# State-space stage: the heads' products in pairs on the two column halves, and another order of ScalarE's and VectorE's work behind each group

## The reference, cut to what matters

```python
CB = einsum('btgn,bsgn->btsg', C_c, B_c)
y_intra = einsum('btsg,btsgh,bsgh,bsghp->btghp', CB, L, dt_c, x_c)
y_inter = einsum('btgn,bghpn,btgh->btghp', C_c, state, exp(cum))
...
y = y + D_skip * xh
y = y * silu(z)
y = y * rsqrt(mean(y * y over the group) + EPS) * g_out
h = h + y @ w_out
```

## Time and profile before

| what | value |
|---|---|
| median of 3 runs | 1914.03 us (1911.9 to 1917.88) |
| the profiled execution | 1913.78 us, of which its span is 1912.0 us |
| busy in the span | PE 1800.4 us (94%), DVE 989.7 (52%), ACT 789.6 (41%), POOL 711.9 (37%) |
| the state-space stage | from 80 to about 520 us of the span |
| chain that ended last | PE 76%, DVE 14%, ACT 5%, issue 3% |

### The profile page before, as it was taken

The page is one execution under the profiler, slowest core; times in us unless marked ns, Lnnn a source line. Parts: engine busy times, 40 slices in busy tenths (PEclk is TensorE's granted clock), DMA queues, the critical chain, the costliest instruction groups (busy, mean ns, idle before and its releaser), DMA issues.

```text
span 1912.0 us, 24962 instructions
## 1 busy us (share of the span) xinstructions
PE 1800.4 (94%) x8907; PEld 1426.5 (75%) x8907; DVE 989.7 (52%) x1549; ACT 789.6 (41%) x1341; POOL 711.9 (37%) x795
## 2 busy tenths in 40 slices
PE   5999898998899988999999999999989989999998
PEld 3877776766677655777877878888778768888887
DVE  5658578366634686345656846667631342122122
ACT  4435334344445666335553235544542342223231
POOL 0644444332435210531112432222324545555553
PEclk8999999999999899999999999999999989999999
DMA  5332331211122200211105832121123223333333
GB/s 164 94 101 88 97 113 56 65 49 62 44 81 78 61 23 12 80 45 34 34 23 181 262 108 55 34 56 45 45 67 92 85 72 100 93 99 99 97 90 99
DMA packets 238794, 152.04 MB, mean 80 GB/s; under 512 B 7997, under 2 KB 223046, under 8 KB 238694
## 3 DMA queue, kind: packets, MB, share of 16 engines
q1 hardware_dynamic: 225894, 125.54, 23.1%
q10 hardware_dynamic: 12800, 25.17, 4.0%
HBM read 148.59 MB, written 2.10 MB: 79 GB/s over the span
## 4 chain that ended last, share of the span: by engine, by line
PE 76%; DVE 14%; ACT 5%; issue 3%; DMA 1%; POOL 0%; SPq 0%; DVEq 0%; ACTq 0%; POOLq 0%
PE ps L636 19%; PE ps L640 19%; PE ps L637 19%; PE ps L2004 2%; DVE xs L1241 2%; PE ps L1986 1%; PE ps L1487 1%; PE ps L1519 1%; PE ps L667 1%; PE ps L1993 1%; PE ps L2447 1%; PE ps L918 1%; DVE al L748 1%; DVE queries L1756 1%; DVE mod_part L1262 1%
## 5 line engine op out<-in xcount | busy, mean ns | idle before, releaser
L586 POOL TENSOR_TENSOR wl<-raw,wh 128x256 fp32r<-128x256 f32 (+1 forms) x775 | 688.3, 917 | 1137.9 <-ACT wh L599 1137.9
L636 PE MATMUL ps<-ah,wh 128*128 128x512 f32 (+1 forms) x1208 | 493.3, 408 | 32.6 <-DVE al L748 13.3
L640 PE MATMUL ps<-ah,wl 128*128 128x512 f32 (+1 forms) x1208 | 477.0, 395 | 0.0
L637 PE MATMUL ps<-al,wh 128*128 128x512 f32 (+1 forms) x1208 | 476.3, 394 | 0.0
L599 ACT ACTIVATE wh<-raw 128x1024 fp32r<-128x1024 f32 (+1 forms) x220 | 230.8, 1049 | 345.2 <-PE ps L640 330.8
L636 PEld LDWEIGHTS ps<-ah,wh 128*128 128x128 f32 (+1 forms) x1208 | 229.0, 190 | 104.5 <-issue 39.9
L640 PEld LDWEIGHTS ps<-ah,wl 128*128 128x128 f32 (+1 forms) x1208 | 228.6, 189 | 52.5 <-issue 0.8
L637 PEld LDWEIGHTS ps<-al,wh 128*128 128x128 f32 (+1 forms) x1208 | 229.5, 190 | 46.3 <-issue 1.2
L636 PE MATMUL ps<-bh,wh 128*128 128x512 f32 (+1 forms) x588 | 235.8, 401 | 14.1 <-DVE resid L1352 9.9
L637 PE MATMUL ps<-bl,wh 128*128 128x512 f32 (+1 forms) x588 | 232.1, 395 | 0.0
L640 PE MATMUL ps<-bh,wl 128*128 128x512 f32 (+1 forms) x588 | 231.8, 394 | 0.1
(11 more groups left out here) (372 smaller groups left out, 2621.9 us busy)
## 6 DMA issues: line engine op xcount, KB each, us to landing
raw<-w_mlp SPq DMA_DIRECT2D x64, 512.0 KB, 3.8
raw<-w_in SPq DMA_DIRECT2D x52, 512.0 KB, 3.8
raw<-ssm_w_in SPq DMA_DIRECT2D x40, 512.0 KB, 3.8
ada_late<-w_ada ACTq DMA_DIRECT2D x16, 1024.0 KB, 6.5
ada_raw<-w_ada ACTq DMA_DIRECT2D x16, 512.0 KB, 3.6
raw<-ssm_w_out SPq DMA_DIRECT2D x16, 512.0 KB, 3.4
raw<-mla_w_in SPq DMA_DIRECT2D x11, 512.0 KB, 3.9
raw<-mla_w_out SPq DMA_DIRECT2D x8, 512.0 KB, 3.5
```

Source lines behind the costliest of these rows:

```text
L586: nc.gpsimd.tensor_tensor(wl[:, s, part], raw[:, s, part], wh[:, s, part].bitcast(F32), ALU.subtract).then_inc(lo_ready, LOW_PIECES * (par ...
L636: nc.tensor.matmul(dst, w_hi[k], x_hi[k], start=k == 0, stop=False)
L637: nc.tensor.matmul(dst, w_hi[k], x_lo[k], start=False, stop=False)
L640: ins = nc.tensor.matmul(dst, w_lo[k], x_hi[k], start=False, stop=k == n - 1)
```

## The change

The outputs of two heads are made together: one call for each pair, at odd h, whose five steps each issue the product of the even head and then that of the odd head, so that neighbouring products use different column halves. `seg` and `carry` get a second pair of buffers, in memory that is free in these groups. ScalarE's exponentials of pair p now wait for the outputs of pair p - 2. VectorE takes pair (h - 3) / 2 at h = 3, 5 and 7, instead of pair h / 2 - 1 at h = 2, 4 and 6.

Behind a group, ScalarE first copies P6's result to `zs` as it is and makes the high part of P8's weights, then the squares and the rstd; Silu of the copy comes later, in place; the gate of P7's result and the split behind it move ahead of the four high parts. VectorE's residual add of an output product's first half waits for that half alone (`half_done`), and in the last group the first of these adds stands ahead of the wait for the rstd. At the start of the stage one semaphore is replaced by another.

```diff
@@ pe_mamba
-            def outputs(g, h):
-                pair, part = h // 2, slice(HP * (h % 2), HP * (h % 2) + HP)
...
-                pe.wait_ge(sem("mix_ready"), g * GH + h + 1)
...
+            def outputs(g, pair):
+                b = 6 + pair % 2
+                pe.wait_ge(sem("y_taken"), g * 4 + max(pair - 1, 0) + AHEAD)
+                pe.wait_ge(sem("mix_ready"), g * GH + 2 * pair + 2)
+                for step in range(5):
+                    for two in range(2):
+                        h, part = 2 * pair + two, slice(HP * two, HP * two + HP)
...
+                ins_.then_inc(sem("y_ready"), 1)
@@ output on TensorE
+                    if c == 0:
+                        ins_.then_inc(sem("half_done"), 1)
@@ heads on TensorE
-                    outputs(g, h)
+                    if h % 2:
+                        outputs(g, h // 2)
@@ heads on ScalarE
-                    act.wait_ge(sem("y_ready"), g * GH + max(h - 1, 0) + AHEAD)
+                    act.wait_ge(sem("y_ready"), g * 4 + max(h // 2 - 1, 0) + AHEAD)
@@ act_mamba
             for g in range(GROUPS - 1):
                 heads(g)
+                act.wait_ge(sem("gated"), g * 4 + 1)
+                act.wait_ge(unit_done, unit("ssm", g, 6) + 1 + CREDIT)
+                nc.scalar.activation(zs[:, 0], bank(0), ACT.Copy).then_inc(acc_free[0], 1)
+                split_ahead(act, "ssm", g, 6)
                 for p in range(4):
                     square(g, p)
-                split_ahead(act, "ssm", g, 6)
                 scale(g)
-                gate("ssm", g, g + 1, 0)
+                act.wait_ge(acc_free[0], g * 9 + ACC0["ssm"][0] + 5)
+                nc.scalar.activation(zs[:, 0], zs[:, 0], ACT.Silu)
+                gate("ssm", g, g + 1, 1)
+                split_ahead(act, "ssm", g, 7)
                 for p in range(4):
                     high(g, p)
-                gate("ssm", g, g + 1, 1)
-                split_ahead(act, "ssm", g, 7)
@@ heads on VectorE
-                    if h % 2 == 0 and h:
-                        take(h // 2 - 1)
+                    if h % 2 and h >= 3:
+                        take((h - 3) // 2)
@@ normed on VectorE
+                if between is not None:
+                    between(0)
                 dve.wait_ge(sem("grstd"), g * 2 + 2)
                 for p in range(5):
-                    if between is not None and 1 <= p <= 2:
-                        between(p - 1)
+                    if between is not None and p == 2:
+                        between(1)
@@ output on VectorE
-                dve.wait_ge(unit_done, unit(stage, i, n0 + w) + 1 + CREDIT)
                 for c in range(2):
+                    dve.wait_ge(*((unit_done, unit(stage, i, n0 + w) + 1 + CREDIT) if c else
+                                  (sem("half_done"), 4 * (i if stage == "ssm" else GROUPS - 1) + w + 1)))
```

More of the change, by code:

```diff
@@ L268, in _build @@
                    for k, a in enumerate((fixed.at, fixed.at + DC * P * 4, b_at + 14 * T * 4))]
+        cl_at = fixed.at
         cl = fixed("cl", [P, DC, CTX], F32R)
@@ L495, in _build, with of_head @@
         carry = r("carry", [P, 2, SSM_CHUNK])
+        segs, carries = [seg], [carry]
+        for name, a in (("bl", b_at + 8 * T * 4), ("cl", cl_at)):
+            r2 = Region(a, a + 4 * T * 4)
+            segs.append(r2("seg_" + name, [P, 2, 2 * CW]))
+            carries.append(r2("carry_" + name, [P, 2, SSM_CHUNK]))
+        def of_head(buffers, g, h):
+            pair, two = divmod(h, 2)
+            return buffers[0 if pair % 2 == 0 else 1 if g < 2 else 2][:, two]
         r2 = Region(b_at + 4 * T * 4, b_at + 8 * T * 4)
@@ L908, in exponents @@
                 ins_.then_inc(sem("sums_ready"), 1)
-            def outputs(g, h):
-                pair, part = h // 2, slice(HP * (h % 2), HP * (h % 2) + HP)
-                b, own = 6 + pair % 2, slice(h * HP, (h + 1) * HP)
-                if h % 2 == 0:
-                    pe.wait_ge(sem("y_taken"), g * 4 + max(pair - 1, 0) + AHEAD)
-                pe.wait_ge(sem("mix_ready"), g * GH + h + 1)
[L917 to L924, removed]
+            def outputs(g, pair):
[5 more added lines that the diff above has]
+                        h, part = 2 * pair + two, slice(HP * two, HP * two + HP)
+                        own, z = slice(h * HP, (h + 1) * HP), of_head(segs, g, h)
+                        if step == 0:
+                            nc.tensor.matmul(bank(b, part, slice(0, W0)), xdt[:, 0, own], z[:, 0:W0], start=True, stop=False)
+                        elif step == 1:
+                            nc.tensor.matmul(bank(b, part, slice(P, W0)), xdt[:, 1, own], z[:, W0:CW], start=False, stop=True)
+                        elif step == 2:
+                            nc.tensor.matmul(bank(b, part, slice(W0, T)), xdt[:, 2, own], z[:, CW:CW + W0], start=True, stop=False)
+                        elif step == 3:
+                            nc.tensor.matmul(bank(b, part, slice(W0 + P, T)), xdt[:, 3, own], z[:, CW + W0:2 * CW], start=False, stop=False)
+                        else:
+                            ins_ = nc.tensor.matmul(bank(b, part, slice(W0, T)), state[:, own], of_head(carries, g, h), start=False, stop=True)
+                ins_.then_inc(sem("y_ready"), 1)
@@ L1003, in act_mamba @@
         def act_mamba(act):
[L1005 removed]
+            act.wait_ge(acc_free[0], ACC0["dt"][0] + 2)
             nc.scalar.activation(dt_e[:], dt_u[:], ACT.Abs).then_inc(sem("dt_act"), 1)
@@ L1048, in heads @@
                         k, cols = j // 2, (slice(0, W0), slice(W0, CW))[j % 2]
-                        nc.scalar.activation(seg[:, h % 2, k * CW + cols.start:k * CW + cols.stop], bank((b0, b1)[k])[:, cols],
+                        nc.scalar.activation(of_head(segs, g, h)[:, k * CW + cols.start:k * CW + cols.stop], bank((b0, b1)[k])[:, cols],
                                              ACT.Exp, bias=ncum[:, j, g * GH + h:g * GH + h + 1])
-                    nc.scalar.activation(carry[:, h % 2].rearrange("p (k n) -> p k n", n=P), ps[:, b0:b1 + 1, CW:T],
+                    nc.scalar.activation(of_head(carries, g, h).rearrange("p (k n) -> p k n", n=P), ps[:, b0:b1 + 1, CW:T],
                                          ACT.Exp).then_inc(sem("seg_ready"), 1)
@@ L1187, in dve_mamba @@
             dve.wait_ge(unit_done, unit("dt", 0, 0) + 1 + CREDIT)
-            nc.vector.tensor_scalar(dt_u[:], bank(0, slice(0, NH)), ssm_a[:, 0:1], None, ALU.add).then_inc(sem("dt_u"), 1)
-            dve.wait_ge(sem("dt_u"), 1)
-            dve.sem_inc(acc_free[0], 1)
+            nc.vector.tensor_scalar(dt_u[:], bank(0, slice(0, NH)), ssm_a[:, 0:1], None, ALU.add).then_inc(acc_free[0], 1)
+            dve.wait_ge(acc_free[0], ACC0["dt"][0] + 2)
             dve.wait_ge(sem("dt_act"), 4)
@@ L1300, in take @@
                 def take(pair):
-                    dve.wait_ge(sem("y_ready"), g * GH + 2 * pair + 2 + AHEAD)
+                    dve.wait_ge(sem("y_ready"), g * 4 + pair + 1 + AHEAD)
                     nc.vector.scalar_tensor_tensor(xs[:, pair], xs[:, pair], dcol[:, g * 4 + pair:g * 4 + pair + 1], bank(6 + pair % 2),
@@ L1310, in heads @@
                     dve.wait_ge(sem("seg_ready"), g * GH + h + 1)
-                    nc.vector.tensor_tensor(seg[:, h % 2], seg[:, h % 2], cb[:], ALU.mult)
-                    nc.vector.tensor_tensor(carry[:, h % 2], carry[:, h % 2], ct[:, SSM_CHUNK:T], ALU.mult).then_inc(sem("mix_ready"), 1)
-                    if h % 2 == 0 and h:
-                        take(h // 2 - 1)
+                    z, c = of_head(segs, g, h), of_head(carries, g, h)
+                    nc.vector.tensor_tensor(z, z, cb[:], ALU.mult)
+                    nc.vector.tensor_tensor(c, c, ct[:, SSM_CHUNK:T], ALU.mult).then_inc(sem("mix_ready"), 1)
+                    if h % 2 and h >= 3:
+                        take((h - 3) // 2)
                     if g < CTX_BLOCKS // 2:
@@ L1392, in last_of_group @@
             def last_of_group(c):
-                if c:
-                    dve.wait_ge(unit_done, unit("ssm", GROUPS - 2, 13) + 1 + CREDIT)
+                dve.wait_ge(*((unit_done, unit("ssm", GROUPS - 2, 13) + 1 + CREDIT) if c else (sem("half_done"), 4 * (GROUPS - 1))))
                 nc.vector.tensor_tensor(resid[:, 6 + c], resid[:, 6 + c], bank(c), ALU.add).then_inc(acc_free[c], 1)
```

## The result

| | before | changed | ratio, 95% interval |
|---|---|---|---|
| median | 1913.68 us (1911.9 to 1917.88, 4 runs) | 1886.88 us (1883.59 to 1887.34, 4 runs) | 0.9853, 0.9834 to 0.9873 |
| profiled execution | 1913.78, span 1912.0 | 1883.59, span 1881.8 | |

The change gained 26.8 us by the medians and 30.2 by the two profiled executions, against a forecast of 28.1. The profiled execution of the changed kernel is the fastest of its four, 3.3 us under their median, so its parts add up to more than the medians show. Lines of the changed kernel are 12 to 27 higher: L648 to L652 are the projections, L932 to L940 the heads' products, L877 `turn_x`, L1379 the residual add.

What follows compares the result with a forecast made beforehand. Bounds taken: TensorE's issue in the heads of groups 0 to 2, VectorE's queue in their tails, a three-engine ring in group 3. Terms -7.0, -7.0, -6.2, -7.9 give -28.1: 1913.8 to 1885.7 us, range 1878 to 1896.

Steps and rivals of the forecast that it cites:

- Part 1: Heads' products in groups 0 to 2: a pair of heads costs 1.88 us, the price of one; -7.2 us per group.
- E: Heads' products: the column halves do not overlap and the heads lose their present neighbour's gain; 1911 us, chance 0.05.
- F: Heads' products: each change of column half costs 0.15 us, so the kernel is slower, 1956 us; chance 0.04.
- the wait for the mix: TensorE's wait for a pair's odd head in groups 0 to 2: costed at nothing, since the projections cover it.
- rival C: Heads of groups 0 and 1: VectorE bounds them, reaching the last take late; up to +7, 1893 us; chance 0.16.
- Part 2: ScalarE behind groups 0 to 2: 6.9 us less waiting gains nearly nothing; later high parts cost +0.3, +0.3, +0.4 us.
- Part 3: Adds by halves: -0.9, -0.9, -0.3 us in groups 0 to 2; -2.3 at the end, of it -1.7 in ssm_last.
- Part 4: Group 3's heads: ScalarE's exponentials no longer wait for outputs 0 and VectorE becomes the bound; -5.6 us.
- Part 5: TensorE's clock behind longer waits in the tails of groups 0 to 2: +0.8, +0.8, +0.9 us; 0 at the end.
- Rival B: TensorE's clock: no half-speed stretch behind the tails (-2.5 us) and none behind 490 (-3.5); 1879.7 us, chance 0.14.

Runs made afterwards that it cites:

- e3: Changed kernel, but within a pair the five products of the even head come first, then the five of the odd head: 1903.94 us, ratio to before 0.9941.
- e5: Changed kernel with only one pair of buffers for seg and carry, exponentials of pair p waiting for outputs of pair p - 1: 1906.91 us, ratio to before 0.9947.
- e2: Kernel before the change with ScalarE's new order and the adds by halves, outputs still head by head: 1912.55 us, ratio to before 0.9994.
- e4: Changed kernel with ScalarE's order behind a group put back as before the change: 1882.1 us, ratio to before 0.9832.
- e1: Changed kernel with only the pairs, their buffers and VectorE's order of takes kept; ScalarE's order and adds as before the change: 1889.71 us, ratio to before 0.987.
- e10: e8 with VectorE's sums of squares in ssm_last moved behind the next unit's first add: 1873.52 us, ratio to before 0.9774.
- e6: Changed kernel with ScalarE's four high parts ahead of Silu of the copy and the gate of P7's result: 1877.82 us, ratio to before 0.9793.
- e9: Changed kernel with 22, 15 and 22 unneeded matmuls behind output product 0 of groups 0, 1 and 2: 1883.58 us, ratio to before 0.9816.
- e8: Changed kernel with ScalarE's old order, output product 0 added before the fourth convolution in three tails, group 2's output product 1 before turn_x: 1868.32 us, ratio to before 0.9754.

## Why the prediction was right, point by point

| us | forecast | measured in the profiles |
|---|---|---|
| heads, groups 0 to 2 | -7.2 each | -7.11, -7.14, -7.14 |
| group 3, heads | -5.6 | -5.05 |
| high parts later | +0.3, +0.3, +0.4 | +0.35, +0.37, +0.45 (tails) |
| adds by halves and clock, groups 0 to 2 | -0.1, -0.1, +0.6 | -1.29, -0.11, -0.11 (rest) |
| end: adds, ssm_last, clock | -2.3 | -2.17 |
| elsewhere | 0 | -1.2 |
| sum | -28.1 | -30.2 |

The main term, 21.6 of the 28.1 us, was right in mechanism and in size. Of the small terms several were off, and they cancelled in part; that the sum came out within 2.1 us owes something to luck.

**Part 1** held to 0.1 us: a pair costs 1.88 us, the price of one head; rivals E and F are out (F's own terms give +48 us and not +46, which changes nothing). The attention stage's loop told it before the change was built, and e3 shows that the order of the loop makes it. The rule of the Trainium skill ("TensorE: Matmul & The Clock Gate", Part 3, The mechanism), strict program order of matmuls, does not describe these runs: in e3 a pass of the odd head begins at 126.12, ahead of three of the even head that stand before it in the program.

That the wait for the mix costs nothing held too, in the changed kernel; rival C did not come: VectorE waited 1.03 us for the outputs of pair 3, where I had left it 0.5 us of room. e5 shows how thin the cover is in the pairs: my "more than 10 us" between a head's sums and the outputs that need them is true of pairs 1 and 2, but for pair 3 it is 8.3 us (from 152.2 to 160.5 in the changed kernel).

**Part 2** held, and e2 and e4 show it from both sides. Removing 6.9 us of waits gave nothing, since VectorE's queue set the end; the later high parts cost 0.4 to 0.6 us in each tail. The changed kernel's timeline has the hole:

```profile
173.32 1.41 DVE L1366 SCALAR_TENSOR_TENSOR norm_v<-xs,vec,rstd 128x512 f32<-128x512 f32 x2
175.48 0.81 DVE L1370 TENSOR_TENSOR bl<-norm_v,bh 128x512 fp32r<-128x512 f32 x1 [0.76 <-ACT bh L1095]
```

VectorE waits 0.76 us for the first high part. Before, this queue had none.

**Part 3** held for the tails and came out right at the end by luck. The wait for `xw` went from 1.3 to 0.7 us. At the end, the add ahead of the rstd gave 0.5 us where I had 0.6. Of the four waits in ssm_last two are left, but they are longer than the old ones: 1.3 and 1.0 us. TensorE's waits there, before (499 to 521 us) and in the changed kernel (426 to 500 us):

```profile
PE ps L636 <- DVE resid L1352: 2.6, 3, 0.9
PE ps L636 <- issue: 0.8, 1, 0.8
```

```profile
PE ps L648 <- DVE bl L1370: 3.3, 3, 2.2
PE ps L648 <- ACT wh L611: 1.3, 1, 1.3
PE ps L648 <- issue: 1.0, 1, 1.0
```

So 1.1 us of 3.4 went, not 1.7 of 3.5. Two of the three waits for `bl`, 0.8 and 0.3 us, lie inside the first output product and are new; with them TensorE waits as long in ssm_last as before. What made this stretch 1.7 us shorter is the clock, for which I had taken nothing here:

```profile
463.00:477.30 14.30, 13.07 (x48) 9.82 (x48) 9.81 (x16) 6.82 (x9) 7.01 (x8) 0.88 0.11 37
```

Without its waits TensorE takes 13.1 us for the first two output products. Before it took 14.7, of which 9.0 went to the first at a clock of 0.64. e1 has this gain of the clock without the adds, and its end is 0.8 us shorter than before; from e1 to the changed kernel it is 1.3 us more. So the adds by halves gave 1.3 us here, not 2.3. e10 shows that the reason I gave for the two waits left is right: with the sums moved, both are gone.

**Part 4** was 0.6 us off. The first mix of group 3's second pair took 1.45 + 0.94 us instead of 0.96 + 0.42, while GpSimd made a low part; that is 1.0 us, and the 0.4 us of small waits that I had allowed did not come:

```profile
440.06 1.45 DVE L1335 TENSOR_TENSOR seg_cl<-seg_cl,cb 128x768 f32<-128x768 f32 x1 [1.98 <-ACT carry_cl L1071]
441.43 0.94 DVE L1336 TENSOR_TENSOR carry_cl<-carry_cl,ct 128x256 f32<-128x256 f32 x1
442.30 0.94 DVE L1335 TENSOR_TENSOR seg_cl<-seg_cl,cb 128x768 f32<-128x768 f32 x1
```

GpSimd's four operations ran from 438.6 to 442.1 us. All 32 mixes of the changed kernel fit this: the 14 whose first product (`seg`) ran while GpSimd did nothing took 0.94 to 0.96 us for it, and of the 18 that overlapped one of its operations 16 took 1.2 to 1.5 us. No run moved GpSimd's work, so the cause is not shown by itself.

**Part 5** had the mechanism and not the size. I took +0.8, +0.8 and +0.9 for the clock; parts 3 and 5 together came to -1.3, -0.1 and -0.1. By the starts of passes, `turn_x` fell from 3.15 to 2.55 us and `turn_b` from 3.36 to 2.84 (in group 2 from 3.76 to 3.25), so the adds gave -1.1, -1.1 and -0.5, and the clock about -0.2, +1.0 and +0.4: 1.2 us where I had 2.5. At the end it gave -1.7 where I had 0. What I did not see is how much the slow clock cost in all, before as well as after: 1.4, 2.6 and 1.0 us in the changed kernel (rest against e6 or e9 at full speed). e6 got all of it back, e9 in groups 0 and 2, e8 in groups 0 and 1. Rival B's argument, that every wait of over 2.5 us is followed by a slow stretch, holds in the trace before the change and fails in e5 and e6, behind waits of 3.4 and 2.8 us.

## What to carry to other kernels

Products that use half of the array's columns should alternate between the halves in the order of the program; two that follow each other in blocks overlap only at the seam. Before work is moved to end a wait, ask which queue ends last behind it: here 6.9 us of waits were worth nothing, and moving one add ahead of one convolution was worth 2.9 us in each of two tails. A wait on the way to the same bound can be worth having where it splits a long one: in e6 TensorE went on at full speed behind it. And a sum that comes out right is checked term by term: the end of the stage was forecast to 0.1 us by two errors that cancelled.

## What the runs showed of the hardware that I had not expected

A pass for the other column half starts ahead of passes that stand before it in the program, but only when few of them are left: three in e3, three before the change (at 160.20, ahead of those at 160.30, 160.41 and 160.63).

Behind the waits of 3 to 6 us at the end of the tails TensorE went on at 1.2 GHz for a while (in the changed kernel the granted clock was 0.50 from 417.7 to 421.1 us, behind the wait for `xs`), and matmuls put into the wait, useful to nobody, kept the clock at 2.4 GHz (granted 1.00 instead of 0.78 behind it). Which waits have this effect is open; e5, e6 and e8 show some of 2.2 to 3.4 us that had none.

The scatter between whole executions goes with the same clock. The attention stage, unchanged, in the changed kernel and in e3:

```profile
523.20:736.00 212.80, 196.14 (x1002) 139.41 (x1002) 133.94 (x300) 123.24 (x295) 56.85 (x59) 0.98 0.16 47
```

```profile
540.30:759.00 218.70, 202.06 (x1002) 142.27 (x1001) 133.88 (x299) 123.24 (x295) 56.84 (x59) 0.95 0.16 46
```

The same 1002 passes take 5.9 us longer at a mean granted clock of 0.95 instead of 0.98, with VectorE and ScalarE busy for the same time. So a kernel's profile can differ from another's by 6 us in a stage that neither touched. The twelve profiles agree: "later" took 1389.6 to 1392.8 us in the nine whose mean granted clock there was 0.985 to 0.987, and 1396.8, 1397.7 and 1399.3 in e10, e9 and e3, where it was 0.982, 0.980 and 0.979. What moves the clock from one execution to the next is not shown.
